# A two-block transformer on one core: paired steps of the modulation product, shift and scale chunks taken in turn, first rows modulated by twos, sums in four column groups

## The reference, cut to what matters

```
silu_c, silu_cc = silu(c), silu(c_ctx)
for l in range(2):                                    # first block
    mod_x = silu_c  @ w_ada[l] + b_ada[l]             # 1024 -> 6 * 1024
    mod_c = silu_cc @ w_ada[l] + b_ada[l]
    sh1, sc1, gt1, sh2, sc2, gt2 = split(mod, 6)      # for x and for ctx
    hx = rms_norm(x, g_norm1[l]) * (1 + sc1_x) + sh1_x
    hc = rms_norm(ctx, g_norm1[l]) * (1 + sc1_c) + sh1_c
    q, k, v of three kinds = hx @ w_in[l], hc @ w_in[l]
    three kinds of attention, w_out, residual with gt1,
    norm and modulation with sh2 and sc2, gated FFN with a 3-tap
    convolution over the tokens, residual with gt2
for l in range(2):                                    # second block
    h = rms_norm_2(x, ...)                            # "pre"
    four branches, gates, w_out, x = x + rms_norm_2(., post)
    gated FFN, x = x + rms_norm_2(f, norm_ffn_post)   # "fpost"
```

## Time and profile before

| | |
|---|---|
| median of 3 runs | 2297.65 us (2296.98 to 2303.8) |
| profiled execution | 2298.63 us |
| its span | 2296.8 us |
| TensorE busy | 2151.5 us, 94% |
| VectorE busy | 1532.2 us, 67% |
| ScalarE busy | 1152.5 us, 50% |
| GpSimd busy | 565.1 us, 25% |
| read from HBM | 374.42 MB, 163 GB/s over the span |

### The profile page before, as it was taken

One profiled execution on the slowest core, in us unless ns is written; L12 is line 12 of the kernel. 1 busy time (PEld: TensorE's weight loads), 2 busy tenths in 40 slices (PEclk: granted clock), 3 DMA queues, 4 the chain that ended last, 5 costly groups with the idle time before them and its releaser, 6 DMA issues.

```text
span 2296.8 us, 42538 instructions
## 1 busy us (share of the span) xinstructions
PE 2151.5 (94%) x17528; PEld 1987.3 (87%) x17528; DVE 1532.2 (67%) x2285; ACT 1152.5 (50%) x1917; POOL 565.1 (25%) x668
## 2 busy tenths in 40 slices
PE   6999989999999998989998989999998998999997
PEld 4985668999999995679997979999997888998997
DVE  3657766777777765757777678855555777965554
ACT  3533444554655552555556546554444655564443
POOL 0021330333233102213321043213331124312331
PEclk8998999999999997999999999999999999999999
DMA  8535454555465453435563525554553443454552
GB/s 326 165 129 202 154 196 156 175 194 183 148 204 190 148 165 115 162 110 191 189 195 99 165 93 189 173 171 147 186 188 109 143 146 132 166 175 141 189 193 83
DMA packets 103200, 378.22 MB, mean 165 GB/s; under 512 B 11584, under 2 KB 11744, under 8 KB 101984
## 3 DMA queue, kind: packets, MB, share of 16 engines
q1 hardware_dynamic: 101520, 367.31, 47.2%
q10 hardware_dynamic: 1488, 8.20, 0.9%
HBM read 374.42 MB, written 1.05 MB: 163 GB/s over the span
## 4 chain that ended last, share of the span: by engine, by line
PE 36%; issue 8%; DVE 5%; POOL 3%; ACT 3%; POOLq 0%; DVEq 0%; ACTq 0%
PE ps L395 11%; PE ps L397 10%; PE ps L396 10%; DVE WL L1577 2%; POOL R L2539 1%; PE ps L454 1%; POOL R L2497 1%; ACT WH L967 1%; DVE RST L1613 1%; PE ps L409 1%; DVE R L1587 1%; PE ps L410 1%; PE ps L417 1%; DVE TMP L1587 1%; POOL X L2300 0%
## 5 line engine op out<-in xcount | busy, mean ns | idle before, releaser
L395 PE MATMUL ps<-X,WH 128*128 128x256 f32 x4384 | 1241.8, 283 | 16.9 <-DVE WL L1577 16.0
L396 PE MATMUL ps<-X,WH 128*128 128x256 f32 x4384 | 1227.9, 280 | 0.0
L397 PE MATMUL ps<-X,WL 128*128 128x256 f32 x4384 | 1226.1, 280 | 0.0
L1577 DVE TENSOR_TENSOR WL<-RAW,WH 128x1024 fp32r<-128x1024 f32 (+2 forms) x608 | 782.5, 1307 | 455.3 <-ACT WH L967 454.6
L395 PEld LDWEIGHTS ps<-X,WH 128*128 128x128 f32 x4384 | 826.2, 188 | 31.5 <-DVE WL L1577 21.2
L396 PEld LDWEIGHTS ps<-X,WH 128*128 128x128 f32 x4384 | 826.6, 189 | 1.4
L397 PEld LDWEIGHTS ps<-X,WL 128*128 128x128 f32 x4384 | 826.4, 188 | 0.0
L967 ACT ACTIVATE WH<-RAW 128x1024 fp32r<-128x1024 f32 (+2 forms) x608 | 624.1, 1046 | 270.5 <-PE ps L397 263.5
L1105 ACT ACTIVATE PB<-ps,SM 128x512 f32<-128x512 f32 (+1 forms) x152 | 87.8, 584 | 165.4 <-DVE SM L1747 165.1
L2342 POOL TENSOR_SCALAR R<-CONS,SM 128x128 f32<-128x128 f32 x128 | 84.4, 670 | 351.0 <-DVE SM L1757 351.0
L2436 POOL TENSOR_TENSOR TMP<-TMP 128x256 f32<-128x256 f32 x66 | 49.0, 743 | 445.2 <-ACT TMP L1289 445.2
(11 more groups left out here) (188 smaller groups left out, 2257.1 us busy)
## 6 DMA issues: line engine op xcount, KB each, us to landing
RAW<-w_dram SPq DMA_DIRECT2D x674, 512.0 KB, 3.9
RAW<-w_dram SPq DMA_DIRECT2D x16, 480.0 KB, 3.2
BIG<-big_dram ACTq DMA_DIRECT2D x4, 1024.0 KB, 5.1
RAW<-w_dram SPq DMA_DIRECT2D x8, 320.0 KB, 2.7
RAW<-w_dram SPq DMA_DIRECT2D x6, 384.0 KB, 3.1
XT<-x_dram ACTq DMA_DIRECT2D x2, 1024.0 KB, 10.7
CONS<-con_dram ACTq DMA_DIRECT2D x1, 1105.0 KB, 4.9
out_dram<-XT SPq DMA_DIRECT2D x1, 1024.0 KB, 3.9
```

Of the source, the lines that this page charges most:

```text
L395: e.matmul(out, a.hi, b.hi, start=start and i == 0, stop=False, skip_group_check=open_bank)
L396: e.matmul(out, a.hi, b.lo, start=False, stop=False, skip_group_check=open_bank)
L397: last = e.matmul(out, a.lo, b.hi, start=False, stop=stop and i == n - 1, skip_group_check=open_bank)
L1577: e.tensor_tensor(weights(i).lo, raw(i), weights(i).hi.bitcast(F32), ALU.subtract).then_inc(*w_lo.mark(i))
```

## The change

1. **A step takes half a bank row, two steps share one turn.** A step is now 16 matmuls of 128 columns (32 records) into four groups of 32 partitions: two groups for each half of the 256 outputs. SCZ is 34 columns wide, and the second step of a pair reads it two columns further left (`CVEC`), so its results land in rows 2 and 3 of each group while the first step's stand in rows 0 and 1. After the second step there is one copy of 128 columns (before: one of 256 columns for each step), one `pick` matmul with 8 columns (before: four matmuls for two steps), and one or two additions of b_ada. All steps now use the one bank `k.ada`, and `ada_turn` is called before each new pair.
2. **Order of the first eight steps.** FIRST = [0, 4, 1, 5, 2, 6, 3, 7]: shift and scale of the same 256 features are neighbours, and make a pair.
3. **Rows modulated as they come.** The squares are taken after step 3. Tiles 0 to 3 are scaled after the second pair, then two tiles after each further pair, each with its own gain instruction.
4. **No early splits.** The first steps are called with `ahead` = 0. Transfer 16 (the first split one) is split by ScalarE before step 7, by VectorE after the last scaling; transfer 17 and the next are issued at the first projection.
5. **Transfers asked for later.** The first parameters (215 columns, with `lam` moved ahead of the convolution weights) and 265 columns of constants, then XT of stream 0. XT of stream 1, the rest of the constants, the rest of the parameters and the positions are asked for after the last high part, before BIG. The wait on s_par2 moves to `conv_gate`.
6. **Sums in groups.** For x0, "fpost" and "pre" the squares go through ones[:, 0:32] into four groups of 32 partitions, four tiles at a time. ScalarE copies the bank (Copy), one more matmul with the constant `four` adds the groups, and the root is taken of that.

```diff
-CONSTS = [("ident", 128), ("ones", 128), ("eps", 1), ("pick", 2), ("sel", 256), ...
+CONSTS = [("ones", 128), ("eps", 1), ("pick", 8), ("four", 128), ("ident", 128), ("sel", 256), ...
+FIRST = [0, 4, 1, 5, 2, 6, 3, 7]
...
-        SCZ = R[:, 7168:7424].rearrange("p (k m) -> p k m", k=8)
+        SCZ = R[:, 7168:7440].rearrange("p (k m) -> p k m", k=8)
+        CVEC = [SCZ[:, :, 2 - 2 * step:34 - 2 * step] for step in range(2)]
...
# TensorE, SquareSum.flush, and rstd
+                    while len(self.pend) >= 4 + keep:
...
+                        for x in range(4):
+                            b, _ = self.pend.pop(0)
+                            e.matmul(self.bank.ap[32 * x:32 * x + 32, 0:256], ones[:, 0:32], b.ap, start=self.i == 0,
+                                     stop=self.i == self.total - 4).then_inc(*sums.mark(self.tag, self.i + x))
...
+                        q.wait_ge(*parted(self.tag))
+                        e.matmul(self.bank.ap[:, 256:512], con("four"), out.ap, start=True, stop=True)...
...
# TensorE, ada_turn and ada_step
-                for h in range(2):
-                    last = e.matmul(bank.ap[:, 256 + 2 * h:258 + 2 * h], b.ap[:, 128 * h:128 * h + 128], con("pick"), start=True, stop=True)
-                last.then_inc(*adaturn.mark(l, c))
+                e.matmul(bank.ap[:, 256:264], b.ap[:, 0:128], con("pick"), start=True, stop=True).then_inc(*adaturn.mark(l, c))
...
-            def ada_step(ring=PS, ahead=3):
+            def ada_step(ring=k.ada, ahead=3):
...
+                step = int(k.first is not None)
+                if not step:
+                    ada_turn()
+                    k.first = (l, c), ring.take()
...
-                    for c4 in range(4):
-                        last = e.matmul(bank.ap[32 * c4:32 * c4 + 32, 0:256], SCZ[:, 4 * h + c4], w[:, c4], start=h == 0, stop=h == 1)
+                    for n in range(2):
+                        for x in range(4):
+                            c4 = 2 * (x // 2) + n
+                            last = e.matmul(bank.ap[32 * x:32 * x + 32, 0:128], CVEC[step][:, 4 * h + c4], w[:, c4, 128 * (x % 2):128 * (x % 2) + 128], ...)
...
# TensorE, start
-                ada_step(PS, NRAW)
+                ada_step(PS, 0)
                 if c == 4:
+                    ss.rstd(k.rst[0])
+                if c % 2:
+                    ada_turn()
+                if c == 3:
                     ss = SquareSum("x0", 8)
...
# ScalarE, start
+            high, rest = modulate(("n1", 0, 0), 0, 0, X[0], lag=0)
             for c in range(8):
+                if c == 7:
+                    feed.reach(17)
+                ada_step(PS, 0)
+                if c == 3:
                     ss = SquareSum("x0", 8)
...
+                if c > 1 and c % 2:
+                    for n in range(4) if c == 3 else (c - 1, c):
+                        high(n)
...
+            e.dma_start(XT[:, 1], x_d[:, 1]).then_inc(s_c, 16)
+            e.dma_start(CONS[:, 265:ncon], con_d[:, 265:ncon]).then_inc(s_con2, 16)
+            e.dma_start(PARS[:, 215:npar], par_d[:, 215:npar]).then_inc(s_par2, 16)
+            e.dma_start(posb, pos_d).then_inc(s_pos, 16)
             e.dma_start(BIG[:], big_d[0]).then_inc(s_big, 16)
...
# VectorE, ada_step and start
-                e.tensor_copy(b.ap, bank.ap[:, 0:256]).then_inc(*modded.mark("row", l, c))
+                if step:
...
+                    e.tensor_copy(b.ap[:, 0:128], bank.ap[:, 0:128]).then_inc(*modded.mark("row", *place))
...
+                ada_step(PS, 0)
+                if c > 4 and c % 2:
+                    rest(0 if c == 5 else 4), rest(1 if c == 5 else 5)
+                if c % 2:
+                    ada_turn()
+                if c == 3:
                     SquareSum("x0").rstd(k.rst[0])
+                if c > 1 and c % 2:
+                    for n in range(4) if c == 3 else (c - 1, c):
+                        scaled_by(n)
+                if c == 5:
+                    rest(2), rest(3)
+            feed.reach(17)
+            rest(6), rest(7)
```

More of the change, by code:

```diff
@@ L127, in room, with reach @@
         return before < 0 or self.halves[before] in self.back
-    def next(self, ahead=NRAW):
-        i = self.n
-        self.n += 1
-        while self.cut < min(i + ahead, self.total) and self.room():
+    def reach(self, end):
+        while self.cut < min(end, self.total) and self.room():
             if self.cut in self.place:
@@ L135, in next @@
             self.cut += 1
-        return i
+    def next(self, ahead=NRAW):
+        self.n += 1
+        self.reach(self.n - 1 + ahead)
+        return self.n - 1
     def release(self, i):
@@ L457, in rstd @@
                     self.flush()
+                    if self.grouped:
+                        q.wait_ge(*parted(self.tag))
+                        e.matmul(self.bank.ap[:, 256:512], con("four"), out.ap, start=True, stop=True).then_inc(*sums.mark(self.tag, "all"))
                     self.bank.free = [roots(self.tag)]
@@ L1022, in rstd, with ada_step @@
                     wait(out.free)
-                    e.activation(out.ap, self.bank.ap[:, 0:256], ACT.Sqrt, scale=1.0 / size, bias=eps).then_inc(*roots.mark(self.tag))
-            def ada_step(ring=PS, ahead=3):
-                k.todo.pop(0)
-                ring.take()
+                    total = self.bank.ap[:, 0:256]
+                    if self.grouped:
+                        e.activation(out.ap, total, ACT.Copy).then_inc(*parted.mark(self.tag))
+                        q.wait_ge(*sums(self.tag, "all"))
+                        total = self.bank.ap[:, 256:512]
+                    e.activation(out.ap, total, ACT.Sqrt, scale=1.0 / size, bias=eps).then_inc(*roots.mark(self.tag))
+            def ada_step(ring=k.ada, ahead=3):
+                k.todo.pop(0)
+                if k.first is None:
+                    ring.take()
+                    k.first = True
+                else:
+                    k.first = None
                 used(ahead)
@@ L1043, in rest @@
                     bufs[c].free = [x_lo(tag, c)]
+                if not lag:
+                    return high, rest
                 return staged(8, high, *[lambda c: None] * (lag - 1), rest)
@@ L2617, in rows, with ada @@
             put(w[c:c + 128 * k])
-    def ada(w):
-        for c in range(0, w.shape[1], 256):
+    def ada(w, order=None):
+        for c in [256 * c for c in order or range(w.shape[1] // 256)]:
             put(w[:512, c:c + 256], False)
@@ L2752, in constants @@
     put("eps", EPS)
-    put("pick", np.tile(np.eye(32)[:, 0:2], (4, 1)))
+    put("four", (p % 32 == 0)[:, None])
+    pick = np.zeros((2, 2, 32, 2, 2, 2))
+    for step, half, st in np.ndindex(2, 2, 2):
+        pick[:, half, 2 * step + st, step, half, st] = 1.0
+    put("pick", pick.reshape(128, 8))
     sel, selT = np.zeros((128, 4, 2, 32)), np.zeros((128, 4, 128))
```

118 lines of the change are left out of this document (68 added, 50 removed).

## The result

The changed kernel takes **2258.43 us** (median of 4 runs, 2251.98 to 2268.02) against 2297.32 (4 runs, 2293.89 to 2303.8): ratio 0.9831, 95% interval 0.9801 to 0.9862, 39 us less. The forecast was 2275, in 2261 to 2288. The sign is right, and the gain is 16 us larger than the sum of 23. All runs of both kernels are in the same, faster state of the chip.

What follows compares the result with a forecast made beforehand. It took a waiting start and attention units in which every TensorE instruction counts as the bounds. Gains of 7 (start), 13 (other steps) and 3 us (sums) from 2298.63 gave 2275.6, 2275 against medians; forecast range 2265 to 2284, 8-in-10 range 2261 to 2288.

Steps and rivals of the forecast that it cites:

- the sum of 23: Whole kernel: gains of 7 us (start), 13 us (other 40 steps) and 3 us (sums of squares) added together.
- Start: Start of the kernel: low pass of the first projection ends at 45.8 against 52.81, gain 7 us, bounds 2 and 12.
- the named waits: Start: pair 2's copy waits behind VectorE's scalings, first splits come late; stream 1's XT hidden by 5 us.
- I take 1.10, so 0.30 net: Each of the other 40 steps: 0.40 us saved in the turn, step itself 1.10 instead of 1.00 us.
- the term of the other 40 steps: Attention and `norm_qk`: 34 steps give 10.2 us, six save waits worth 3; gain 13 us, bounds 5 and 20.
- (d): Attention: the lower clock spreads, nine more units go from 4.86 to about 8 us, costing 28: 2303 us; chance 4%.
- Granted clock of 175 to 300 still near 0.90: Sign for the attention stage: TensorE's granted clock in that window stays near the 0.90 of before.
- (a): Start gives nothing: serial pairs, VectorE holding pair 2 and late transfer 17 cost 7 us more: 2282 us; chance 12%.
- (b): Steps give nothing: 16 added loads stand in the open, 0.52 us a step: 2293.6, half open 2288; chance 12%.
- (c): Steps paced by their records at 53 ns, 1.70 us instead of 1.00: 2313 us; chance 4%.
- (e): Whole kernel: more than expected, waits and second bank hand-overs vanish too: 2258 us; chance 6%.
- Sums: Grouped sums of squares: 1.2 us for each "fpost", 0 to 0.5 for "pre"; gain 3 us, ends 0 and 4.

## Why the prediction was right and wrong

**Start: right.** Forecast 7 in 2 to 12, measured 7.6 in the mean of the profiles (5.4 to 11.2 between single ones), with the named waits (pair 2 behind the reciprocal and the scalings, the late splits of transfers 16 and 17, nothing lost by stream 1's late XT). Not foreseen was that neither half of the change, the new start or the pairs, pays in the start without the other.

**Steps: mechanism right, size wrong.** "I take 1.10, so 0.30 net": a step of 32 records took 1.01, so 0.10 was set aside for nothing, while the products gave 0.67 a pair, not 0.81; the two errors nearly cancel, and units at the high level gave 0.39 a step. The step that failed is the term of the other 40 steps, 13 us where 28.2 were measured: it took all lengths from rows at the high level, and carried's granted clock of 0.90 only into rival (d), as something that can get worse. It went the other way, 0.92 to 0.98 in stage A. That is some 10 of the missing 15 us, by what is left and not by a test of the clock alone; some 3 come from 0.39 instead of 0.30 a step, and some 2 from the normalisation. "Granted clock of 175 to 300 still near 0.90" was the line that would have shown it; the window of the same code has 1.00.

**Rivals.** (a) did not come; the late splits and the wait of pair 2 came when the forecast's own chain had them. (b) is refuted by the loads: 32 of them take 0.81 us inside the 1.01 of the step. By the sentence of the Trainium skill ("TensorE: Matmul & The Clock Gate", The mechanism) that loads overlap with running matmuls only where the row group differs, all 16 added loads would stand in the open; the trace does not agree. (That section of the Trainium skill also lets loads into a background weight buffer go ahead of running matmuls; no run here tells whether that is what happens.) The prediction's own argument against (b) had a wrong reading in it: the 0.85 us that stand there for the streaming of a step are the loads of another product (L607). (c) falls by the same row as (b). (e) came true in time, 2258, by a cause that it did not name: not more vanished waits alone, but the clock; that its number was met is luck. (d) did not come: the prediction had a lighter stage lose clock. The Trainium skill ("TensorE: Matmul & The Clock Gate", What's actually happening), which it named there, ties the clock to how busy the array was; TensorE was busy 0.92 of stage A before and after, and the clock rose, so the mean busy share does not tell this change of the clock.

**Sums:** about 1.6 us for the two "fpost" instead of 2.4, inside the ends of the term.

## What to carry over

When a stage shows a granted clock under 1.00, the clock is a term of the sum with both signs: read how long the low level lasts in the stage, and price its going as well as its coming. Look for edits that need each other (here pairs want a start without early splits): the trace of one part alone can even be slower. And before filling idle time to hold the clock, see whether the pass behind it is bound by TensorE at all.

## What was not expected of the hardware

- A product with 128-column weights and 2 or 8 streamed columns costs TensorE 0.22 us in a closed chain of work, in both directions measured; splitting each product of 256 columns into two of 128 on other column groups costs nothing that shows (1.00 before, 1.01 us after for a step).
- The low clock moves from run to run in unchanged code: up to the ninth split seven profiles of the same start took 62.6 to 67.4 us, and the changed kernel's four runs 2252 to 2268. Single profiles of this kernel should not be read closer than 5 us in the start and 1 to 4 us in a stage.
- 3.73 us of dead products in 4.9 us of idle time cut a low stretch of 10.2 us to 3.4, and it was worth 0.5 us at most.
- A us at the low level cost 0.35 us in a unit of attention (4.19 us against 2.71).
